# Gate and up projections: the low parts of two token operands of each run, made by GpSimd instead of VectorE

## The chip, the cores and the metric

The kernel runs on one core of a Trainium2 chip. The metric is the device time of one execution, in microseconds (us); less is better.

## The reference, cut to what matters

The reference is one layer of a hybrid decoder: a 2048-token prompt and eight single decode tokens go through a combined projection, three groups of heads, an output projection, and a SwiGLU feed-forward block. Everything is in float32. The change lies in the first half of the feed-forward block:

```python
def swiglu(h, w_gate, w_up, w_down):
    return (jax.nn.silu(h @ w_gate) * (h @ w_up)) @ w_down
```

Here `h` has 2056 rows (2048 prompt tokens and 8 decode tokens) of 1024, and `w_gate` and `w_up` are 1024 x 2816.

## The kernel before, in words

The kernel is a row of stages: `project_all`, `attend`, `combine`, `gate_up`, `down`. Each stage has one instruction stream for each engine, written out by hand, and semaphores between them; an engine works strictly in the order of its stream. A barrier stands between stages.

**Split products.** TensorE multiplies in a reduced float format (F32R). So each operand is split in a high part (a copy rounded by ScalarE) and a low part (the operand minus its high part, by VectorE or GpSimd), and each product is three matmuls: high times high, high times low, low times high.

**Seven products.** `gate_up` computes each 2 x 2 block product with seven smaller products of sums of blocks. They are called, in their order, b11, t2, t3, t1, b21, t4, b22 (m = 0 to 6). Each has a weight operand (a block of 512 x 128, or a combination of blocks) and a token operand. The seven token operands are A11, S2, S3, S1, A12, A22 and a second S2 (the variable `source_of`); S1 to S3 are sums, and the last one, made by the step called s4, overwrites S2. Each token operand is 4 x W columns on 128 partitions, with W = 344, 344 and 340.

**Runs.** The 2056 tokens are worked in three runs of those widths. A run has 22 steps g: gate and up for each of 11 pairs of column blocks. In every step TensorE does 7 products of 12 matmuls. A run's token operands are made once, at its beginning, and used by all its 22 steps. The first run's are made in the opening of the stage; those of the second and third run at a turn, in the last step of the run before (g = 21 and g = 43; `turn` in VectorE's stream).

**What each engine does in a step.** ScalarE makes the high parts of the next step's weights (`base_hi`, L2435 and L2436, and `combos_hi`, L2426) and copies the first product out (L2465). At a turn it also makes the seven high token parts (`tokens_hi`, L2451), the seventh after s4. VectorE makes low parts of weights (`combos_lo`, L2488, and `base_lo`, L2498), adds the products up (L2548, L2554, L2565, and L2510 in `quarter`), multiplies gate and up (L2514), and makes sums for the next stage (`act_sums`, L2523 to L2531); at a turn it makes the seven low token parts between these (`tokens_lo`, L2503). GpSimd makes the rest of the low weight parts (`base_lo`, L2403), the weight combinations of the step after next (`combos`, L2390, L2391, L2393, L2395), and at a turn then s4 (L2324). SyncE issues the loads and the stores.

TensorE waits, in the first step of a run (`i == 0`), for the low token part of each product. VectorE's order at a turn is: low part 0, quarter t1, low part 1, quarter b21 with its sums, low part 2, quarter t4 with its sums, low part 3, quarter b22 with its sums, low parts 4, 5 and 6. In the opening it is: low part 0, weights, low parts 1, 2, 3, then s4 (on VectorE this time), low parts 4, 5, 6; GpSimd does `combos(1)` meanwhile.

Of the kernel before, what the change touches and what calls it, by code (L numbers as in the profile page):

```python
# [14 lines left out]
F32 = mybir.dt.float32  # L15
# [3 lines left out]
ALU = mybir.AluOpType  # L19
# [980 lines left out]
def attend(nc, c, a, io, scratch, dec, key_of, cache, last_page, y_first, first_root):  # L1000
# [12 lines left out]
    units, items, phase_of, phase_start = [], {}, {}, []  # L1013
    slot = 0
    for own, work in attention_phases():
        span = len(own) or len(work) + 3
        phase_start.append((slot, len(units)))
        units_at = len(units)
        for after, item in work:
            items.setdefault(slot + after, []).append(item)  # L1020
            phase_of[item] = units_at
        if not own:
            first_unit = slot + span
        units += own
        slot += span
# [100 lines left out]
    with ExitStack() as ctx:  # L1126
# [4 lines left out]
        names = ("low_zeroed in_turned q_copied0 q_copied1 q_copied2 q_copied3 k_hi in_hi in_lo turned t_hi t_lo pv scored min made probs v_hi v_lo o_copied o_ready inverted o_out row_made row_out "  # L1131
                 "q0 q1 k0 k1 v0 v1 decay page0 page1 page2 weighed halved added st0 st1 st2 st3 row_st0 row_st1 "
                 "raised conv_w_in conv_in0 conv_in1 conv_step conved conv_out w_ahead gain_ahead fox_ahead mem_ahead first_squares first_var first_root first_normed")
        with stage(nc, names) as (block, s):
# [11 lines left out]
            for n in range(SLOTS_ALL):  # L1146
                m = unit_at(n)
# [6 lines left out]
                if u:  # L1154
                    k = chunk_index[u.head, u.ch]
# [459 lines left out]
def combine(nc, c, io, scratch, dec, first, y_first, first_root, stock):  # L1615

    N = NT + 1
    SAMP = NT  # L1620
# [531 lines left out]
WIDTHS = (344, 344, 340)  # L2152
# [84 lines left out]
def gate_up(nc, c, io, scratch, raw, stock):  # L2237
# [14 lines left out]


    SC, ITEMS, M = len(WIDTHS), 2 * PAIRS, len(ORDER)
    N = SC * ITEMS
    W = max(WIDTHS)
    H = DT // 2
    with ExitStack() as ctx:
        sb, psum = alloc(ctx, nc)
        h_hi, h_lo = sb("h_hi", [P, M, H, W], F32R), sb("h_lo", [P, M, H, W], F32R)  # L2260
# [5 lines left out]
        last_out = last_results(stock)  # L2266
        ps = psum("ps_gate_up", [P, 8, BLK])
        source_of = (A11, S2, S3, S1, A12, A22, S2)
        names = ("w_in0 w_in1 t_step t_made t_hi t_lo b_hi b_lo d_lo a11_in h_in s_step h_hi h_lo b_first done p1 u2 u3 u4 c22 c11 c21 c12 silu "
                 "quarter summed act stored sum_stored s_stored ahead")  # L2270
        with stage(nc, names) as (block, s):
            w_in = (s.w_in0, s.w_in1)
# [25 lines left out]
            def product(g, name):  # L2298
                return ps[:, (M * g + ORDER.index(name)) % 8, 0:width(g)]

            def shape(ap):
                return ap.rearrange("p m d n -> p (m d) n")

            def s_combo(eng, sc, name):

                n = WIDTHS[sc]
                x = [part[:, i, :, 0:n] for i in range(6)]
                step = 4 * sc - 3
                if name == "s1":
                    eng.wait_ge(s.h_in, 48 * sc)  # L2310
                    eng.wait_ge(s.a11_in, 16 * sc)
                    eng.tensor_tensor(x[S1], x[S3], x[A22], ALU.add).then_inc(s.s_step, 1)
                elif name == "s2":
                    eng.wait_ge(s.s_step, step + 1)
                    eng.tensor_tensor(x[S2], x[S1], x[A11], ALU.subtract).then_inc(s.s_step, 1)
                elif name == "s3":
                    eng.wait_ge(s.s_step, step + 2)
                    eng.tensor_tensor(x[S3], x[A11], x[S3], ALU.subtract).then_inc(s.s_step, 1)
                else:

                    if sc:
                        eng.wait_ge(s.s_step, step + 3)
                    eng.wait_ge(s.h_lo, M * sc + 2)
                    eng.tensor_tensor(x[S2], x[A12], x[S2], ALU.subtract).then_inc(s.s_step, 1)  # L2324

            @block.sync
            def _(sp):
                def weights(g):
                    if g >= N:
                        return  # L2330

                    if g >= 3:
                        sp.wait_ge(s.b_lo, g - 2)
                    sp.wait_ge(s.d_lo, g - 1)
                    sp.dma_start(raw[:, g % 2], gate_up_weights(io, g)).then_inc(w_in[g % 2], 16)

                def tokens(sc):

                    sp.wait_ge(s.h_lo, M * sc)
                    if sc == SC - 1:  # L2340
                        sp.wait_ge(c.last_h, LAST_STORES)
                    load_tokens(sp, scratch, stock, sc, s.a11_in, s.h_in)

                def down_ahead():

                    pile, acts, _ = down_buffers(stock)
                    sp.wait_ge(s.h_lo, M * SC)
                    for j in range(PILE):
                        sp.dma_start(pile[:, j, :], down_rows(io.w_down)[:, 0, j, 0:BLK]).then_inc(s.ahead, 16)
                    sp.dma_start(acts[0], scratch.act_c[KEPT.index(PASSES[0]), 0]).then_inc(s.ahead, 16)  # L2350

                for g in range(N):
                    if g == 0 or is_up(g):
                        weights(g + 2)
                    if is_up(g):
                        weights(g + 3)
                    if g % ITEMS == 2 and g // ITEMS + 1 < SC:
                        tokens(g // ITEMS + 1)
                    if g == 2 * ITEMS + 9:
                        sp.wait_ge(s.stored, stored_before(2 * PAIRS))  # L2360
                        sp.wait_ge(s.sum_stored, stored_before(2 * PAIRS))
                        down_ahead()
                    if is_up(g) and g < N - 1:
                        j = g % ITEMS // 2
                        sp.wait_ge(s.act, g // 2 + 1)
                        for p, at, t, n in run_pieces(g // ITEMS):
                            dst = scratch.act_c[0:3, p, :, j, at:at + n].rearrange("m p t -> p m t")
                            sp.dma_start(dst, sums_of(g)[:, :, t:t + n]).then_inc(s.sum_stored, 16)
                        for p, at, t, n in run_pieces(g // ITEMS):
                            dst = scratch.act_c[3:7, p, :, j, at:at + n].rearrange("m p t -> p m t")  # L2370
                            sp.dma_start(dst, out_of(g)[:, :, t:t + n]).then_inc(s.stored, 16)
                        if g // ITEMS == SC - 1:
                            sp.dma_start(scratch.act_s[:, j].rearrange("p s (a t) -> p (s a) t", a=2),
                                         act_out[:, :, all_but_sample(g):width(g)]).then_inc(s.s_stored, 16)
                sp.wait_ge(s.stored, stored_before(N // 2 - 1))
                sp.wait_ge(s.sum_stored, stored_before(N // 2 - 1))
                sp.wait_ge(s.s_stored, 16 * (PAIRS - 1))
                sp.wait_ge(s.ahead, 16 * (PILE + 1))

            @block.gpsimd  # L2380
            def _(pool):
# [15 lines left out]
                def base_lo(g):  # L2397
# [4 lines left out]
                    at = SLOT["b11"]  # L2402
                    pool.tensor_tensor(shape(lo[:, at:at + 2]), b[:, :, 0:P], shape(hi[:, at:at + 2]).bitcast(F32), ALU.subtract).then_inc(s.b_lo, 1)  # L2403

                combos(1)
                for g in range(N):
                    base_lo(g + 1)
                    combos(g + 2)
                    sc, i = g // ITEMS + 1, g % ITEMS
                    if sc < SC:  # L2410
                        if i in (8, 12, 16):
                            s_combo(pool, sc, ("s1", "s2", "s3")[(i - 8) // 4])
                        if i == ITEMS - 1:
                            s_combo(pool, sc, "s4")

            @block.scalar
            def _(act):
# [65 lines left out]
            def _(dve):  # L2483
# [14 lines left out]
                    dve.tensor_tensor(w_lo[:, g % 2, last], raw[:, g % 2, H:DT, P:2 * P], w_hi[:, g % 2, last].bitcast(F32), ALU.subtract).then_inc(s.d_lo, 1)  # L2498

                def tokens_lo(sc, m):  # L2500
                    n = WIDTHS[sc]
                    dve.wait_ge(s.h_hi, M * sc + m + 1)
                    dve.tensor_tensor(h_lo[:, m, :, 0:n], part[:, source_of[m], :, 0:n], h_hi[:, m, :, 0:n].bitcast(F32), ALU.subtract).then_inc(s.h_lo, 1)  # L2503

                def quarter(g, name, base, which, read):

# [28 lines left out]
                combos_lo(0)  # L2535
                dve.tensor_tensor(w_lo[:, 0, SLOT["b22"]], raw[:, 0, H:DT, P:2 * P], w_hi[:, 0, SLOT["b22"]].bitcast(F32), ALU.subtract).then_inc(s.d_lo, 1)
                tokens_lo(0, 1)
                tokens_lo(0, 2)
                tokens_lo(0, 3)
                s_combo(dve, 0, "s4")  # L2540
                for m in range(4, M):
                    tokens_lo(0, m)
                for g in range(N):
                    n, b, q = width(g), g % 2, g // 2
# [25 lines left out]
                    quarter(g, "b21", first[:, b, 0:n], 0, s.c11)  # L2570
                    if is_up(g):
                        act_sums(g, 0)
                    if turn:
                        tokens_lo(turn, 2)
                    quarter(g, "t4", u3[:, 0:n], 1, s.c21)
                    if is_up(g):
                        act_sums(g, 1)
                    if turn:
                        tokens_lo(turn, 3)
                    dve.wait_ge(s.u4, g + 1)  # L2580
                    quarter(g, "b22", u2[:, b, 0:n], 2, s.c12)
                    if is_up(g):
                        act_sums(g, 2)
                    if turn:
                        for m in range(4, M):
                            tokens_lo(turn, m)

            @block.tensor
            def _(pe):
                for g in range(N):  # L2590
# [7 lines left out]
                    for m, name in enumerate(ORDER):  # L2598
# [2 lines left out]
                        if g == 0 and name == "b22":  # L2601
                            pe.wait_ge(s.d_lo, 1)
                        if i == 0:
                            pe.wait_ge(s.h_lo, M * sc + m + 1)
                        if m == 0 and g >= 2:

                            pe.wait_ge(s.c12, g - 1)
# [525 lines left out]
```

## Time and profile before

| | |
|---|---|
| three timed runs | 2769.03, 2776.25 and 2781.96 us; median 2776.25 us |
| the profiled execution's own time | 2769.61 us |
| its span, first to last instruction | 2767.9 us |
| mean granted TensorE clock | 0.98 |
| the stage `gate_up` in the span | from about 1403 to about 2312 us |

The span lies within 1.7 us of the profiled execution's own time. Times in the rows below are in us from the start of the span, those marked ns apart. A busy engine is one with an instruction in flight, and an instruction's time holds what it waited for once it had begun.

### The profile page before, as it was taken

To read this page: it belongs to the slowest core of one execution; us is meant where nothing else is said; L and a number is where in the kernel's file an instruction comes from. 1 tells how busy PE (TensorE), PEld (TensorE's weight loads), DVE (VectorE), ACT (ScalarE), POOL (GpSimd) and SP (SyncE) were. 2 spreads that over 40 slices of the span, in tenths; PEclk is the share of its full clock that TensorE was granted. 3 is DMA by queue.
4 is the path that set the end of the run, shared out by engine and by line. 5 is a ranking of instruction groups with operands and counts; after the bars stand their busy time and mean duration, and the time that the engine had idled before them with its cause. 6 is when DMAs were issued, how large, how long until landed. Compare 5 with 4: busy or idle time off the path is not lost. (4 is left out here: it accounts for less than half of the span.)

```text
span 2767.9 us, 42326 instructions
## 1 busy us (share of the span) xinstructions
PE 2632.1 (95%) x14745; PEld 2377.2 (86%) x14745; DVE 1935.7 (70%) x2560; ACT 1169.0 (42%) x2012; POOL 1694.4 (61%) x963
## 2 busy tenths in 40 slices
PE   8999989889999998899979999999989999999998
PEld 7999889877777777677879999999989997887887
DVE  5366696478888887676577778878787875445664
ACT  4212321367777777633343333333433332223343
POOL 3486678488999998655556675666666660222232
PEclk9999999989999999999989999999999999999999
DMA  6588789566666677776635433543434546754564
GB/s 210 167 266 253 252 268 319 170 178 169 176 176 172 176 185 194 214 251 197 203 78 182 133 112 115 168 130 113 130 112 129 172 118 191 243 178 168 185 221 141
DMA packets 471365, 499.21 MB, mean 180 GB/s; under 512 B 172123, under 2 KB 359446, under 8 KB 470122
## 3 DMA queue, kind: packets, MB, share of 16 engines
q1 hardware_dynamic: 449730, 469.97, 56.3%
q10 hardware_dynamic: 21136, 25.50, 2.7%
q8 instruction: 118, 1.93, 0.3%
q0 software_dynamic: 288, 1.05, 0.1%
q14 instruction: 93, 0.76, 0.1%
HBM read 398.07 MB, written 94.16 MB: 178 GB/s over the span
## 5 line engine op out<-in xcount | busy, mean ns | idle before, releaser
L2613 PE MATMUL ps_gate_up<-h_hi,w_hi 128*128 128x344 f32 (+1 forms) x1848 | 593.7, 321 | 26.2 <-DVE h_lo L2503 14.2
L2615 PE MATMUL ps_gate_up<-h_hi,w_lo 128*128 128x344 f32 (+1 forms) x1848 | 594.0, 321 | 0.0
L2614 PE MATMUL ps_gate_up<-h_lo,w_hi 128*128 128x344 f32 (+1 forms) x1848 | 593.4, 321 | 0.0
L2613 PEld LDWEIGHTS ps_gate_up<-h_hi,w_hi 128*128 128x128 f32 x1848 | 349.9, 189 | 29.7 <-DVE h_lo L2503 16.4
L2614 PEld LDWEIGHTS ps_gate_up<-h_lo,w_hi 128*128 128x128 f32 x1848 | 350.2, 190 | 0.0
L2615 PEld LDWEIGHTS ps_gate_up<-h_hi,w_lo 128*128 128x128 f32 x1848 | 350.1, 189 | 0.0
L878 PE MATMUL ps_proj<-w_hi,h_hi 128*128 128x428 f32 (+1 forms) x800 | 289.3, 362 | 10.0 <-ACT proj_out L602 9.9
L879 PE MATMUL ps_proj<-w_lo,h_hi 128*128 128x428 f32 (+1 forms) x800 | 285.4, 357 | 0.0
L880 PE MATMUL ps_proj<-w_hi,h_lo 128*128 128x428 f32 (+1 forms) x800 | 284.9, 356 | 0.0
L1595 DVE TENSOR_TENSOR p_lo<-ps_turned,p_hi 128x512 fp32r<-128x512 f32 (+1 forms) x352 | 211.0, 614 | 81.5 <-ACT p_hi L1483 80.0
L2390 POOL TENSOR_TENSOR stock<-common 128x512 f32<-128x512 f32 x65 | 104.2, 1602 | 251.0 <-DVE w_lo L2488 235.9
L3009 PE MATMUL ps_down<-wd_hi,act_hi 128*128 128x512 f32 x616 | 241.6, 392 | 6.3 <-DVE wd_lo L2917 6.3
L2807 POOL TENSOR_TENSOR stock<-common 128x512 f32<-128x512 f32 x55 | 82.1, 1501 | 265.7 <-DMA common<-in_w_down 265.6
L3011 PE MATMUL ps_down<-wd_hi,act_lo 128*128 128x512 f32 x616 | 240.7, 391 | 0.0
L3010 PE MATMUL ps_down<-wd_lo,act_hi 128*128 128x512 f32 x616 | 240.7, 391 | 0.0
L1483 ACT ACTIVATE p_hi<-ps_turned 128x512 fp32r<-128x512 f32 (+1 forms) x352 | 185.8, 538 | 129.0 <-PE ps_turned L1420 91.7
L1420 PE MATMUL ps_turned<-ident,probs 128*128 128x128 f32 x1216 | 195.7, 278 | 25.0 <-DVE p_lo L1595 8.9
L2855 ACT ACTIVATE act_hi<-stock 128x768 fp32r<-128x768 f32 (+2 forms) x114 | 83.1, 774 | 302.5 <-PE ps_down L3011 288.7
L1420 PEld LDWEIGHTS ps_turned<-ident,probs 128*128 128x128 f32 x1216 | 145.8, 142 | 67.1 <-DVE p_lo L1595 16.4
L2403 POOL TENSOR_TENSOR w_lo<-common,w_hi 128x1024 fp32r<-128x1024 f32 x65 | 162.5, 2500 | 64.2 <-ACT w_hi L2436 64.2
L2933 DVE TENSOR_TENSOR acc<-acc,ps_down 128x512 f32<-128x512 f32 x96 | 62.4, 684 | 198.0 <-PE ps_down L3011 198.0
L2488 DVE TENSOR_TENSOR w_lo<-stock,w_hi 128x2048 fp32r<-128x2048 f32 x66 | 165.3, 2504 | 19.2 <-ACT w_hi L2426 19.0
(346 smaller groups left out, 6574.3 us busy)
## 6 DMA issues: line engine op xcount, KB each, us to landing
stock<-in_cache_k SPq DMA_DIRECT2D x192, 256.0 KB, 3.4
common<-in_cache_v SPq DMA_DIRECT2D x172, 256.0 KB, 3.1
stock<-act_combined SPq DMA_DIRECT2D x56, 704.0 KB, 4.2
common<-in_w_gate SPq DMA_DIRECT2D x33, 1024.0 KB, 5.3
common<-in_w_up SPq DMA_DIRECT2D x33, 1024.0 KB
common<-in_w_down SPq DMA_DIRECT2D x44, 512.0 KB, 5.8
page_v<-in_cache_v SPq DMA_DIRECT2D x84, 256.0 KB, 3.1
common<-in_w_in SPq DMA_DIRECT2D x44, 428.0 KB, 4.9
```

Of the source, the lines that this page charges most:

```text
L878: pe.matmul(ps[:, bank, 0:w], a_hi, w_hi[:, d, :], start=(j == 0 and d == 0), stop=False)
L879: pe.matmul(ps[:, bank, 0:w], a_hi, w_lo[:, d, :], start=False, stop=False)
L880: mm = pe.matmul(ps[:, bank, 0:w], a_lo, w_hi[:, d, :], start=False, stop=(j == 3 and d == 1))
L1420: turned = pe.transpose(out[:, r * P:(r + 1) * P], probs(u.head, QCH * u.ch + r, u.j * P, (u.j + 1) * P), c.ident[:])
L1483: act.activation(a.p_hi[:, m % PARTS, r0 * P:], ps_t[:, bank_of["unit", m], r0 * P:], ACT.Copy).then_inc(s.t_hi, 1)
L1595: dve.tensor_tensor(a.p_lo[:, m % PARTS, r0 * P:], ps_t[:, bank_of["unit", m], r0 * P:], a.p_hi[:, m % PARTS, r0 * P:].bitcast(F32), ALU.s ...
L2613: pe.matmul(acc, a_hi, h_hi[:, m, d, 0:n], start=d == 0, stop=False)
L2614: pe.matmul(acc, a_hi, h_lo[:, m, d, 0:n], start=False, stop=False)
L2615: mm = pe.matmul(acc, a_lo, h_hi[:, m, d, 0:n], start=False, stop=d == H - 1)
L3009: pe.matmul(out, a_hi[:, n % 2, j, :], w_hi[:, slot, :], start=first, stop=False)
L3010: pe.matmul(out, a_hi[:, n % 2, j, :], w_lo[:, slot, :], start=False, stop=False)
L3011: mm = pe.matmul(out, a_lo[:, n % 2, j, :], w_hi[:, slot, :], start=False, stop=end)
```

## The change

In each run, the low token parts of the third and fifth product (m = 2 and m = 4, operands S3 and A12) are made by GpSimd in place of VectorE. They get a semaphore of their own, `h_lo_pool`, and whoever waited for `h_lo` with a count now waits for the semaphore and the count that `low_made` gives. At a turn GpSimd does: `combos(g + 2)`, low part 2, s4, low part 4. In the opening it does low parts 2 and 4 ahead of `combos(1)`. VectorE does all its other work in the same order as before.

```diff
-        span = len(own) or len(work) + 3
+        span = len(own) or max(at for at, _ in work) + 4
...
+    POOL_PARTS = (2, 4)
+    DVE_LATE = [m for m in (4, 5, 6) if m not in POOL_PARTS]
...
+            def low_made(sc, m):
+
+                if m in POOL_PARTS:
+                    return s.h_lo_pool, len(POOL_PARTS) * sc + POOL_PARTS.index(m) + 1
+                own = [k for k in range(M) if k not in POOL_PARTS]
+                return s.h_lo, len(own) * sc + own.index(m) + 1
+
+            def low_of(eng, sc, m):
+
+                n = WIDTHS[sc]
+                eng.wait_ge(s.h_hi, M * sc + m + 1)
+                return eng.tensor_tensor(h_lo[:, m, :, 0:n], part[:, source_of[m], :, 0:n], h_hi[:, m, :, 0:n].bitcast(F32), ALU.subtract)
...
-                    eng.wait_ge(s.h_lo, M * sc + 2)
+                    eng.wait_ge(*low_made(sc, 1))
...
-                    sp.wait_ge(s.h_lo, M * sc)
+                    for m in (POOL_PARTS[-1], M - 1):
+                        sp.wait_ge(*low_made(sc - 1, m))
...
+                def tokens_lo(sc, m):
+
+                    low_of(pool, sc, m).then_inc(s.h_lo_pool, 1)
+
+                for m in POOL_PARTS:
+                    tokens_lo(0, m)
                 combos(1)
...
                         if i == ITEMS - 1:
+                            tokens_lo(sc, POOL_PARTS[0])
                             s_combo(pool, sc, "s4")
+                            tokens_lo(sc, POOL_PARTS[1])
...
-                tokens_lo(0, 2)
-                tokens_lo(0, 3)
+                for m in (2, 3):
+                    if m not in POOL_PARTS:
+                        tokens_lo(0, m)
                 s_combo(dve, 0, "s4")
-                for m in range(4, M):
+                for m in DVE_LATE:
                     tokens_lo(0, m)
...
-                    if turn:
+                    if turn and 2 not in POOL_PARTS:
                         tokens_lo(turn, 2)
...
-                        for m in range(4, M):
+                        for m in DVE_LATE:
                             tokens_lo(turn, m)
...
                         if i == 0:
-                            pe.wait_ge(s.h_lo, M * sc + m + 1)
+                            pe.wait_ge(*low_made(sc, m))
```

## Rows read from the trace of the kernel before

**Rows 1.** The page, part 1: busy us, share, instructions of each engine.

```profile
PE 2632.1 (95%) x14745; PEld 2377.2 (86%) x14745; DVE 1935.7 (70%) x2560; ACT 1169.0 (42%) x2012; POOL 1694.4 (61%) x963
```

**Rows 2.** Waits of TensorE, whole span: us in total, times, longest us.

```profile
PE ps_gate_up L2613 <- DVE h_lo L2503: 14.2, 6, 4.0
```

**Rows 3.** Timeline, TensorE, first turn: start, us, work, idle before and releaser.

```profile
1710.12 0.32 PE L2613 MATMUL ps_gate_up<-h_hi,w_hi 128*128 128x344 f32 x1
...
1712.80 0.32 PE L2615 MATMUL ps_gate_up<-h_hi,w_lo 128*128 128x344 f32 x1
1717.07 0.66 PE L2613 MATMUL ps_gate_up<-h_hi,w_hi 128*128 128x344 f32 x1 [3.95 <-DVE h_lo L2503]
1717.53 0.49 PE L2614 MATMUL ps_gate_up<-h_lo,w_hi 128*128 128x344 f32 x1
...
1720.39 0.49 PE L2615 MATMUL ps_gate_up<-h_hi,w_lo 128*128 128x344 f32 x1
1722.72 0.65 PE L2613 MATMUL ps_gate_up<-h_hi,w_hi 128*128 128x344 f32 x1 [1.83 <-DVE h_lo L2503]
...
1732.73 0.40 PE L2613 MATMUL ps_gate_up<-h_hi,w_hi 128*128 128x344 f32 x1 [0.47 <-DVE w_lo L2498]
```

**Rows 4.** Timeline, VectorE, first turn.

```profile
1710.58 0.50 DVE L2510 TENSOR_TENSOR act<-stock,ps_gate_up 128x344 f32<-128x344 f32 x1
...
1712.21 3.30 DVE L2523 TENSOR_TENSOR silu<-act 128x344 f32<-128x344 f32 x1
1715.44 1.58 DVE L2503 TENSOR_TENSOR h_lo<-stock,h_hi 128x1376 fp32r<-128x1376 f32 x1
...
1717.48 0.52 DVE L2514 TENSOR_TENSOR act<-act,silu 128x344 f32<-128x344 f32 x1
...
1718.58 2.58 DVE L2527 TENSOR_TENSOR act<-act 128x344 f32<-128x344 f32 x1
1721.08 1.58 DVE L2503 TENSOR_TENSOR h_lo<-stock,h_hi 128x1376 fp32r<-128x1376 f32 x1
...
1724.66 4.59 DVE L2503 TENSOR_TENSOR h_lo<-stock,h_hi 128x1376 fp32r<-128x1376 f32 x3
...
1731.79 0.68 DVE L2498 TENSOR_TENSOR w_lo<-common,w_hi 128x512 fp32r<-128x512 f32 x1
```

**Rows 5.** Timeline, GpSimd, first turn.

```profile
1709.29 2.52 POOL L2395 TENSOR_TENSOR stock<-common,stock 128x512 f32<-128x512 f32 x1
1711.76 3.38 POOL L2324 TENSOR_TENSOR stock<-stock 128x1376 f32<-128x1376 f32 x1
1718.07 2.71 POOL L2403 TENSOR_TENSOR w_lo<-common,w_hi 128x1024 fp32r<-128x1024 f32 x1 [2.93 <-ACT w_hi L2436]
```

**Rows 6.** Timelines of the opening: ScalarE, VectorE, GpSimd, TensorE.

```profile
1407.62 6.29 ACT L2451 ACTIVATE h_hi<-stock 128x1376 fp32r<-128x1376 f32 x5
...
1410.56 7.84 DVE L2503 TENSOR_TENSOR h_lo<-stock,h_hi 128x1376 fp32r<-128x1376 f32 x3
...
1410.12 1.66 POOL L2390 TENSOR_TENSOR stock<-common 128x512 f32<-128x512 f32 x1 [11.71 <-DVE w_lo L2488]
...
1430.65 0.39 PE L2613 MATMUL ps_gate_up<-h_hi,w_hi 128*128 128x344 f32 x1 [2.15 <-DVE w_lo L2498]
```

**Rows 7.** Timeline, ScalarE, first turn.

```profile
1700.73 6.31 ACT L2451 ACTIVATE h_hi<-stock 128x1376 fp32r<-128x1376 f32 x5
...
1715.18 1.35 ACT L2451 ACTIVATE h_hi<-stock 128x1376 fp32r<-128x1376 f32 x1 [6.29 <-POOL stock L2324]
```

**Rows 8.** Windows (busy us of each engine, then PEclk) and TensorE's first matmul in `down`.

```profile
2019.00:2020.00 1.00, 0.93 (x4) 0.93 (x5) 0.96 (x3) 1.00 (x3) 0.00 (x0) 0.76 0.00 0
2022.00:2023.00 1.00, 0.48 (x2) 0.04 (x1) 1.00 (x1) 0.13 (x1) 0.78 (x1) 0.53 0.00 0
...
2314.17 0.76 PE L3009 MATMUL ps_down<-wd_hi,act_hi 128*128 128x512 f32 x1 [5.00 <-DVE wd_lo L2917]
...
2318.00:2320.00 2.00, 2.00 (x6) 1.51 (x6) 2.00 (x4) 1.11 (x3) 0.00 (x0) 0.53 1.22 266
```

More of the change, by code:

```diff
@@ L2268, in gate_up @@
         source_of = (A11, S2, S3, S1, A12, A22, S2)
-        names = ("w_in0 w_in1 t_step t_made t_hi t_lo b_hi b_lo d_lo a11_in h_in s_step h_hi h_lo b_first done p1 u2 u3 u4 c22 c11 c21 c12 silu "
+        names = ("w_in0 w_in1 t_step t_made t_hi t_lo b_hi b_lo d_lo a11_in h_in s_step h_hi h_lo h_lo_pool b_first done p1 u2 u3 u4 c22 c11 c21 c12 silu "
                  "quarter summed act stored sum_stored s_stored ahead")
@@ L2346, in down_ahead @@
                     pile, acts, _ = down_buffers(stock)
-                    sp.wait_ge(s.h_lo, M * SC)
+                    for m in (POOL_PARTS[-1], M - 1):
+                        sp.wait_ge(*low_made(SC - 1, m))
                     for j in range(PILE):
@@ L2500, in tokens_lo @@
                 def tokens_lo(sc, m):
-                    n = WIDTHS[sc]
-                    dve.wait_ge(s.h_hi, M * sc + m + 1)
-                    dve.tensor_tensor(h_lo[:, m, :, 0:n], part[:, source_of[m], :, 0:n], h_hi[:, m, :, 0:n].bitcast(F32), ALU.subtract).then_inc(s.h_lo, 1)
+                    low_of(dve, sc, m).then_inc(s.h_lo, 1)
                 def quarter(g, name, base, which, read):
@@ L2577, in _ @@
                         act_sums(g, 1)
-                    if turn:
+                    if turn and 3 not in POOL_PARTS:
                         tokens_lo(turn, 3)
```

## The prediction

> **What bounds the kernel now.** I read the page first: TensorE is busy 95% of the span, VectorE 70%, GpSimd 61% [rows 1]. So the time can change only where TensorE waits, or where it runs at the lower clock. The view of TensorE's waits says where that touches the change: six waits for low token parts, 14.2 us together [rows 2], beside a few for low weight parts. The timeline puts them in three places: the opening of the stage (1407 to 1431), the first turn (1713 to 1733) and the second (302 us later, the same instructions with the same durations within 0.1 us). That sum is all that a better placing of this work could give back, with the slow clock that the pauses bring. Within 0.5% (13.9 us) this kernel's runs can't tell a change from none.
>
> At the first turn TensorE has done m = 1 by 1713.1 and starts m = 2 at 1717.07, as soon as VectorE has made its low part (1715.44 + 1.58). It starts m = 3 at 1722.72, after the next low part, and the next step at 1732.73, after VectorE's L2498 [rows 3, 4]. Its matmuls start every 0.158 us at full clock (17 steps from 1710.12 to 1712.80) and every 0.286 us at half clock (10 steps from 1717.53 to 1720.39) [rows 3].
>
> The rows to look at longest are VectorE's L2523 and L2527. Both are subtractions or sums on 344 columns, worth 0.52 us like L2514 [rows 4]. L2523 takes 3.30 us, from 1712.21 to 1715.51, and GpSimd's s4 ends at 1715.14; L2527 takes 2.58 us, to 1721.16, and GpSimd's L2403 ends at 1720.78 [rows 4, 5]. Each ends 0.37 us after the GpSimd instruction. VectorE's L2510, with one input in PSUM, takes 0.50 us in the midst of GpSimd's L2395 [rows 4, 5]. So a VectorE instruction with both inputs in SBUF and a GpSimd instruction exclude each other, for the whole length of the one that has begun, and instructions with a PSUM input go free. GpSimd pays as well: the three low parts of the opening take VectorE 7.84 us beside GpSimd's `combos(1)`, and 4.59 us alone at the turn [rows 4, 6].
>
> The Trainium skill has the same rule (SBUF — State Buffer, Who interferes with whom): a VectorE instruction with two SBUF inputs contends with a GpSimd instruction that reads SBUF, and the one that issues second waits for the other's end. The trace agrees: 3.30 us where 0.52 is the work. The rule speaks against this change, whose moved instruction reads SBUF twice; by it the sum is the one below, and without it the sum would be that of the second rival.
>
> **The moved work and its price.** A low token part is 1.53 us on VectorE (4.59 for three) [rows 4]. GpSimd's price isn't in the rows; the nearest is s4, of the same 128 x 1376 and two SBUF inputs, 3.38 us of which 0.37 was waiting behind L2514: 3.0 us [rows 5]. From L2403, 2.71 us for 1024 columns with a wait of about 0.48 (it began at 1718.07, and L2525 held VectorE until 1718.55), 2.23 us scale to 3.0 too. I take 3.0, with 2.9 and 3.4 as ends. So 3.1 us leave VectorE at each of the three places and 6.0 come to GpSimd, in time that the two share.
>
> **A turn, step by step.** Up to GpSimd's L2395 nothing changes. Then, in us after 1700:
> - GpSimd takes low part 2 where it took s4, its high part being there (ScalarE's five end at 7.0 [rows 7]): 11.8 to 15.1. TensorE starts m = 2 at 15.2 in place of 17.1, a gain of 1.9, and ends it at 17.1 to 18.3, as the clock falls or not.
> - VectorE's L2523 waits as before, to 15.5. GpSimd's s4 gets the port next: 15.5 to 18.5.
> - VectorE now goes on with L2510 (free, to 15.9) and L2514, which waits for s4: it runs 18.5 to 18.9. GpSimd's low part 4: 18.9 to 21.9.
> - VectorE's L2525 waits behind that: 21.9 to 22.2. GpSimd's L2403, whose ScalarE input follows s4's high part (18.5 + 1.35 + 1.0 + 0.5 = 21.4, by [rows 7] and the 2.9 us from L2451 to L2403 in [rows 5, 7]), comes next: 22.2 to 24.5.
> - VectorE's L2527 waits behind that: to 24.8. Low part 3: 24.8 to 26.3. It was there at 22.7 before [rows 4].
>
> TensorE is done with m = 2 by 18.3 and has nothing until 26.4: low part 4 was ready at 21.9, but it belongs to a later product. From 26.4 four products are left, 48 matmuls, 7.6 us at full clock, to 34.0. VectorE meanwhile needs 2.0 us to the next low part, as before (22.66 to 24.66), then two of them where it had three (3.1 in place of 4.6), and ends L2498 at 34.6 where it was 32.5: 2.1 us later [rows 4]. The clock decides which of the two comes last. After a pause of 4.0 us it fell in both turns, and at the beginning of `down`, after 5.0 us, it stayed at half from 2314.2 to about 2319.9 (the window from 2318 has 0.53) [rows 3, 8]. In the second turn it was at half for only about 3.4 us, from 2019.5 to 2022.9 (the mean of 2019 to 2020 is 0.76, that of 2022 to 2023 0.53) [rows 8]. After a pause of 8 us it will be at half: 3.4 us of it cost 3.4 x (1 - 0.158 / 0.286) = 1.5 us, 5.7 us cost 2.55. So TensorE ends the step between 35.5 and 36.5, and the next begins then in place of 32.7: 2.8 to 3.8 us lost. The second turn loses the same. Both together: 5.6 to 7.6.
>
> **The opening.** GpSimd sat idle until 1410.12 [rows 6], so its two low parts look free; they are not. In us after 1400: high part 2 is there at 10.1 (the second of five from 7.6 [rows 6]), and VectorE has a 0.7 us subtraction until 10.6. Then they alternate: GpSimd low part 2, 10.6 to 13.6; VectorE low part 1, to 15.1 (13.3 before, behind L2390, which ended at 11.8); GpSimd low part 4, to 18.1; VectorE low part 3, to 19.6; L2390, to 20.9; VectorE s4, to 22.4; L2391, to 23.6; VectorE low part 5, to 25.1; L2393, to 26.4; VectorE low part 6, to 27.9; L2395, to 29.1. ScalarE's L2426 (1.9 us) needs that last combination: 31.1. Before, `combos(1)` began at 1410.1 and, at some 2.5 us for each of four, was done by 1420, so this was hidden. GpSimd's L2403 holds the port to 31.4, VectorE's L2488 runs to 33.6 and L2498 to 34.2; TensorE starts step 1 at 34.4 in place of 30.65 [rows 6], 3.7 us later, after a pause of over 4 us, with 1.5 to 2.55 of slow clock: 5.2 to 6.3 us lost.
>
> **What costs nothing.** The edit in `attend` changes nothing: the only phase without units has 12 items in slots 0 to 11, so 12 + 3 and 11 + 4 are both 15. SyncE waits twice where it waited once, but for parts long made (the loads of the next run's tokens come two steps into a run). The stores of the turn's results come 3.7 us later; VectorE waits for the first of them before its L2510 of b21 in step 22, some 7 us after L2531. What they need to land no row here shows; if they were late, VectorE's chain has 0.9 to 1.9 us in hand behind TensorE's (34.6 against 35.5 to 36.5). VectorE is busy for 70% of the span [rows 1], so what it is late it catches up in the next steps, but TensorE's loss stays.
>
> **The sum.** 5.2 to 6.3 and 5.6 to 7.6 make 10.8 to 13.9 us; I take 12. Against the profiled execution that is 2769.6 + 12 = 2781.6; against the median of the runs, which lies 6.6 us above it, 2788.
>
> **The rivals.**
> - As summed, with 9 to 16 us: chance 0.60.
> - The clock stays at half through all 48 matmuls of a turn (13.7 us in place of 7.6), or a store or the weight chain adds a wait: 6.1 per turn in place of 1.5 to 2.55, so 18 to 23 us, 2794 to 2799. For it: in the first turn the clock was low from about 1715.7 to 1725.8, through two pauses [rows 3]. Against: it came back in 5.7 us of `down`. Chance 0.17.
> - The other side: GpSimd's new instruction doesn't hold VectorE up. Then at a turn low part 3 is ready before TensorE has done m = 2, s4 ends at 18.2 with its high part at 19.5, L2498 ends by 24.5, and TensorE, going through from 15.2 with five products (9.5 us), starts the next step at 24.7: 8 us gained per turn, up to 3 in the opening, 2757 to 2760. It decides if L2514 and L2525 of the turn take 0.5 us with GpSimd running. [rows 4, 5] are against it. Chance 0.04.
> - The port goes over in another order (VectorE gets two instructions for one of GpSimd's). If L2525 goes straight behind L2514, one wait of 2.2 us goes per turn, low part 3 is there at 24.1, and a turn costs 0.5 to 1.5 us; with less in the opening too, the whole is 2 to 9 us, 2778 to 2785. Against it: where both waited, L2395, L2514, s4, L2523 took turns one by one [rows 4, 5]. Chance 0.15.
> - It makes no difference, as the pause is only split otherwise (within 2 us): 0.04.
>
> **The numbers.** The likeliest case gives 2788. Slower by over 0.5% is above 2790: the second case whole (0.17) and some four tenths of the first (0.25), 0.42 together; faster by over 0.5% is 0.04; the rest, 0.54, is within. For eight in ten, the range goes from the lower edge of the case of the other port order, less 3 for the spread of the medians, 2775, to 2799, the upper edge of the slow-clock case.
>
> **What the profile would show.** TensorE's wait for m = 2 ends near 1715.2 with GpSimd as releaser, and a new wait for VectorE's h_lo of 7 to 9 us begins before m = 3, in both turns. VectorE's L2514, L2525 and L2527 in each turn take 2 to 3.5 us each. GpSimd's low parts take 3.0 to 3.5 us. In the opening `combos(1)` ends near 1429 and the wait for L2498 is 4 us or more. I am wrong if L2525 takes 0.5 us beside GpSimd, or if low part 3 is there before 1724.

## The result and the profile after

Over 20 runs of each kernel the median went from 2769.68 us to 2781.51 us. The ratio is 1.0037, with a 95% interval of 1.0026 to 1.0049: on 2769.7 us that is 10.2 us slower, between 7.2 and 13.6; the two medians lie 11.8 us apart, inside the same interval. The forecast was 12 us slower. Its 2788 was built on a median of three runs, 2776.25; twenty runs put that 6.6 us lower, beside the profiled execution.

The profiled execution of the changed kernel has a span of 2774.1 us, 6.2 us more than before. That isn't the size of the effect either. The view of one line's instructions gives where the stage begins and ends: the first matmul in `gate_up` and the first in `down`. In the kernel before:

```profile
L2613 PE MATMUL ps_gate_up<-h_hi,w_hi x1848: 313/319/656, 1407.3 to 2308.5; 128*128 128x344 f32 x124, 128*128 128x340 f32 x61
L3009 PE MATMUL ps_down<-wd_hi,act_hi x616: 389/389/764, 2314.2 to 2760.0; 128*128 128x512 f32 x154
```

In the changed kernel (24 lines further down):

```profile
L2637 PE MATMUL ps_gate_up<-h_hi,w_hi x1848: 313/319/656, 1402.2 to 2314.9; 128*128 128x344 f32 x124, 128*128 128x340 f32 x61
L3033 PE MATMUL ps_down<-wd_hi,act_hi x616: 389/389/763, 2320.5 to 2766.2; 128*128 128x512 f32 x154
```

The stage was 2314.2 - 1407.3 = 906.9 us long and is 2320.5 - 1402.2 = 918.3 us: 11.4 us more. `down` is as it was (453.7 and 453.6 us to the end of the span), and the stage happened to begin 5.1 us earlier, through stages that the change doesn't touch. Further down, a second profile of each kernel tells how well the stage's length repeats.

TensorE's waits in the stage, changed kernel (us in total, times, longest), beside [rows 2]:

```profile
PE ps_gate_up L2637 <- DVE h_lo L2314: 16.7, 2, 9.0
...
PE ps_gate_up L2637 <- DVE w_lo L2523: 4.2, 1, 4.2
PE ps_gate_up L2637 <- POOL h_lo L2314: 4.1, 2, 2.1
```

Six short waits for low token parts, 14.2 us, have become two long ones, 16.7 us, and two for GpSimd, 4.1 us. The timeline of the first turn, TensorE, VectorE and GpSimd, is what [rows 3 to 5] were before. Everything here is 0.61 us later in the span (1700.58 against 1699.97 for the first sum of step 21). L2314 is the low token part, on either engine; L2537 is the former L2514, L2546 to L2550 the former L2523 to L2527, L2339 is s4, L2420 the former L2403, L2523 the former L2498.

```profile
1715.81 0.42 PE L2637 MATMUL ps_gate_up<-h_hi,w_hi 128*128 128x344 f32 x1 [2.07 <-POOL h_lo L2314]
...
1726.96 0.66 PE L2637 MATMUL ps_gate_up<-h_hi,w_hi 128*128 128x344 f32 x1 [8.98 <-DVE h_lo L2314]
```

```profile
1712.83 3.30 DVE L2546 TENSOR_TENSOR silu<-act 128x344 f32<-128x344 f32 x1
1716.05 0.50 DVE L2533 TENSOR_TENSOR act<-u,ps_gate_up 128x344 f32<-128x344 f32 x1
1716.58 2.90 DVE L2537 TENSOR_TENSOR act<-act,silu 128x344 f32<-128x344 f32 x1
1719.52 3.30 DVE L2548 TENSOR_TENSOR silu<-act 128x344 f32<-128x344 f32 x1
1722.85 2.55 DVE L2550 TENSOR_TENSOR act<-act 128x344 f32<-128x344 f32 x1
1725.32 1.58 DVE L2314 TENSOR_TENSOR h_lo<-stock,h_hi 128x1376 fp32r<-128x1376 f32 x1
...
1734.52 0.69 DVE L2523 TENSOR_TENSOR w_lo<-common,w_hi 128x512 fp32r<-128x512 f32 x1
```

```profile
1712.38 3.37 POOL L2314 TENSOR_TENSOR h_lo<-stock,h_hi 128x1376 fp32r<-128x1376 f32 x1
1715.72 3.39 POOL L2339 TENSOR_TENSOR stock<-stock 128x1376 f32<-128x1376 f32 x1
1719.08 3.37 POOL L2314 TENSOR_TENSOR h_lo<-stock,h_hi 128x1376 fp32r<-128x1376 f32 x1
1722.40 2.63 POOL L2420 TENSOR_TENSOR w_lo<-common,w_hi 128x1024 fp32r<-128x1024 f32 x1
```

Read the last two side by side. GpSimd runs four instructions without a pause. VectorE has four small instructions on 344 columns in the same time, each 0.52 us of work. L2546, L2537, L2548 and L2550 each end 0.37 or 0.38 us after the end of one of GpSimd's: 1716.13 after 1715.75, 1719.48 after 1719.11, 1722.82 after 1722.45, 1725.40 after 1725.03. Only L2533, which reads PSUM, takes its own 0.50 us. Low part 3 is thus ready at 1726.90. TensorE started m = 2 early, finished it, and stood for 8.98 us.

### The profile page after: what moved, and what is told of

Same layout as the page of the kernel before. It is cut to its first block and busy times, and to the rows that moved or that the text cites. A ratio compares the mean times of both kernels' runs of the same rounds, so it can differ in the third digit from the quotient of the medians.

```text
span 2774.1 us, 42328 instructions
## 1 busy us (share of the span) xinstructions
PE 2628.2 (95%) x14745; PEld 2374.9 (86%) x14745; DVE 1943.1 (70%) x2554; ACT 1169.8 (42%) x2012; POOL 1717.0 (62%) x969
## 5 line engine op out<-in xcount | busy, mean ns | idle before, releaser
L2637 PE MATMUL ps_gate_up<-h_hi,w_hi 128*128 128x344 f32 (+1 forms) x1848 | 594.6, 322 | 36.2 <-DVE h_lo L2314 16.7
L2420 POOL TENSOR_TENSOR w_lo<-common,w_hi 128x1024 fp32r<-128x1024 f32 x65 | 160.7, 2472 | 61.4 <-ACT w_hi L2461 61.4
L2460 ACT ACTIVATE w_hi<-common 128x1024 fp32r<-128x1024 f32 x66 | 69.4, 1052 | 254.8 <-PE ps_gate_up L2639 254.8
```

The lines of the kernel that those rows point to most:

```text
L2637: pe.matmul(acc, a_hi, h_hi[:, m, d, 0:n], start=d == 0, stop=False)
```

## The experiments

Each kernel's stage length, from the first matmul of `gate_up` to the first of `down`, is taken from its one profile. It is split at the first sum of step 21 and of step 43 (the line L2548 of before), which lie just ahead of the two turns: 292.7 us, 302.1 us and 312.1 us before. The columns give what each part is longer or shorter than that, from rounded times, so within 0.1 us; the last column is the timed ratio to the kernel before with its 95% interval (twenty runs of the changed kernel, six of the one with the sums late and s4 on VectorE, 10 to 12 of the others).

| kernel | stage, us | opening | first turn | second turn | ratio |
|---|---|---|---|---|---|
| before | 906.9 | | | | |
| before, again | 906.9 | 0.0 | 0.0 | 0.0 | one run |
| changed | 918.3 | +5.7 | +3.2 | +2.5 | 1.0037 (1.0026 to 1.0049) |
| changed, again | 918.1 | +5.6 | +3.2 | +2.4 | one run |
| turns only | 914.0 | +1.6 | +3.2 | +2.4 | 1.0012 (0.9997 to 1.0027) |
| opening only | 913.7 | +5.6 | +1.2 | 0.0 | 1.0010 (0.9994 to 1.0026) |
| part 2 only | 911.9 | +1.8 | +1.6 | +1.6 | 1.0016 (1.0002 to 1.0030) |
| part 4 only | 914.0 | +3.2 | +2.0 | +1.9 | 1.0022 (1.0009 to 1.0034) |
| written only | 901.1 | -0.6 | -3.7 | -1.5 | 0.9965 (0.9951 to 0.9979) |
| s4 on VectorE | 905.0 | +0.1 | -0.9 | -1.1 | 0.9983 (0.9973 to 0.9993) |
| and L2403's work | 902.9 | -0.6 | -1.6 | -1.8 | 0.9983 (0.9969 to 0.9998) |
| sums late | 920.1 | +1.6 | +5.5 | +6.2 | 1.0031 (1.0016 to 1.0047) |
| sums late, s4 on VectorE | 916.8 | 0.0 | +4.3 | +5.5 | 1.0055 (1.0038 to 1.0072) |
| sums at the end, s4 on VectorE | 908.0 | +1.6 | -1.0 | +0.5 | 0.9994 (0.9978 to 1.0011) |

**Both kernels again.** No edit.

> The kernel before unaltered, a second profile: the stage 906.9 us again within 1 us (with the clock's falls placed otherwise, within 2 us), while its beginning (1407 us in the first profile) may move by several us.

> The changed kernel unaltered, a second profile. If the stage's length is a property of the kernel, it is 918.3 us again within 1 us, wherever the stage begins in the span (1402 us in the first profile).

The lengths came back within 0.2 us, 906.9 and 918.1, though the second profile of the changed kernel begins the stage at 1405.2 and not at 1402.2. The stage's beginning lay anywhere between 1400.9 and 1415.3 us over all the profiles of this study, in kernels that are alike up to there. Between the two profiles of the changed kernel the span grew by 4.5 us: 3.0 us of it lie ahead of the stage and 1.7 us in `down`. The stage's length is the sharper measure, but it is one execution of each kernel, and the next experiment shows what the clock can add to it.

**Turns only, opening only.** The set of moved parts is made to depend on the run: none in the first (turns only, shown here), or in the first alone (opening only, `((2, 4), (), ())`).

```diff
-    POOL_PARTS = (2, 4)
+    PARTS = ((), (2, 4), (2, 4))
...
```

The lines left out make the counts and the conditions follow this set.

> GpSimd makes low parts 2 and 4 at the two turns only; the opening is as before. In the profile the gate_up stage (TensorE's first matmul in it to its first in down) was 906.9 us before and 918.3 us with the change. If the three places add up independently, the opening's 5.7 us come back: 912 to 913 us, 5 to 7 us above before in the timed runs, and each turn again has TensorE waiting some 9 and 8 us for low part 3. If instead the loss were one of the whole program (where the code lies, clock, other stages), the stage would stay near 918.

> Low parts 2 and 4 on GpSimd in the opening only; the turns are as before. If the port that VectorE and GpSimd take turns on is the cause, step 1 starts 3 us later than before and then runs at half clock for some us: the stage is 912 to 913 us (906.9 + 5.7). If a GpSimd that was idle costs nothing, as the opening's idle 11.7 us suggest, the stage is 907 us.

Both stages are a little longer than expected, 914.0 and 913.7, and 7.1 + 6.8 is 13.9 and not 11.4. The columns tell why. The turns-only kernel loses 3.2 and 2.4 us at its turns, as the changed kernel does, and the opening-only kernel loses 5.6 us in its opening, as the changed kernel does; these make 11.2 us. What is too much lies where the kernels are unaltered: 1.6 us in the opening of the one, 1.2 us in the first turn of the other. Windows of the turns-only kernel's opening, with PEclk the third number from the end:

```profile
1437.30:1439.30 2.00, 0.64 (x4) 0.67 (x5) 1.97 (x4) 0.00 (x0) 1.24 (x1) 1.00 0.00 0
1439.30:1441.30 2.00, 2.00 (x11) 2.00 (x10) 1.87 (x5) 1.43 (x4) 2.00 (x3) 0.64 0.64 175
1441.30:1443.30 2.00, 2.00 (x9) 2.00 (x9) 0.00 (x0) 2.00 (x4) 1.92 (x2) 0.51 1.00 347
1443.30:1445.30 2.00, 2.00 (x14) 2.00 (x14) 0.52 (x1) 1.96 (x2) 2.00 (x2) 1.00 0.01 2
```

After the pause before step 1 the clock fell to half for about 3.4 us (the means 0.64 and 0.51 of two windows), and the same instructions with the same pause, 2.15 us, kept the full clock in the kernel before. A fall that comes or doesn't is worth about 1.5 us here. The two differ earlier too. This is TensorE's first matmul of m = 1, about 6.1 us into the stage, in the kernel before and in the turns-only kernel:

```profile
1413.33 0.62 PE L2613 MATMUL ps_gate_up<-h_hi,w_hi 128*128 128x344 f32 x1 [2.26 <-issue]
```

```profile
1421.32 0.40 PE L2638 MATMUL ps_gate_up<-h_hi,w_hi 128*128 128x344 f32 x1 [2.26 <-issue]
```

At 0.62 us the clock was still at half there, at 0.40 us it was back at full. Seven profiles have this opening unaltered: the four with 0.62 or 0.63 us kept the stage's opening within 0.1 us of before, the three with 0.40 us (turns only, sums late, sums at the end) lost 1.6 us. What decides when the clock comes back there isn't shown. The timed ratios, 3.3 and 2.8 us with intervals of some 4 us to each side, don't contradict 5.6 and 5.6, but can't confirm them.

**Part 2 only, part 4 only.** The same edit with `((2,), (2,), (2,))` and `((4,), (4,), (4,))`.

> Only low part 2 on GpSimd, everywhere; part 4 stays on VectorE. Taking turns on the port, by durations of the trace: at a turn m = 2 starts 1.9 us earlier, low part 3 is there at about 21.5 (22.7 before), and the next step starts 0 to 1 us later than before; in the opening step 1 starts 2 to 3 us later, with no fall of the clock. Stage 909.5 to 911.5 us, 3 to 4 us above before. If what counts were only how much work GpSimd is given (half of it), it would be half of the change's 11.4 us in the stage: 912.6.

> Only low part 4 on GpSimd, everywhere. By the port theory it is the dearer half although TensorE needs part 4 later: at a turn it comes straight behind s4 and holds up VectorE's low part 2, so m = 2 starts near 20.1 (17.1 before) and low part 3 is there near 25.3 (22.7 before): 1.7 us per turn and up to 1.5 more where the clock stays low; in the opening step 1 starts 2 to 3 us later. Stage 913 to 916 us. By the amount of moved work alone it would be 912.6, as with part 2.

Part 4 alone gave 914.0, inside what was expected; part 2 alone gave 911.9, 0.4 above its upper end. The amount moved is the same, and the losses are 5.0 and 7.1 us. Part 2 missed at the turns: TensorE started m = 3 1.2 us earlier, as expected, but the clock fell in the pause of 4.2 us before it, and the next step began 1.6 us later at the first turn where 0 to 1 was expected, 1.3 us after the low weight parts it needs were ready. Part 4 shows its mechanism in VectorE's timeline of the first turn (L2311 is the low token part there):

```profile
1712.64 3.31 DVE L2545 TENSOR_TENSOR silu<-act 128x344 f32<-128x344 f32 x1
1715.88 4.48 DVE L2311 TENSOR_TENSOR h_lo<-stock,h_hi 128x1376 fp32r<-128x1376 f32 x1
```

GpSimd goes from s4 straight to low part 4, which TensorE needs two products later; VectorE's low part 2, which TensorE is waiting for, takes 4.48 us for 1.5 us of work. TensorE's pause before m = 2 is 6.9 us in place of 3.95, and m = 2 and m = 3 start within 0.2 us of where they were expected.

**Written only.** GpSimd stays as busy, but reads nothing for these parts.

```diff
-                    low_of(pool, sc, m).then_inc(s.h_lo_pool, 1)
+                    pool.wait_ge(s.h_hi, M * sc + m + 1)
+                    for k in range(3):
+                        if k:
+                            pool.wait_ge(s.zeroed, 2 * (2 * sc + (m == 4)) + k)
+                        pool.memset(h_lo[:, m, :, 0:WIDTHS[sc]].bitcast(F32), 0.0).then_inc(s.zeroed if k < 2 else s.h_lo_pool, 1)
```

> In place of low parts 2 and 4 GpSimd writes zeros to them, three times over, so that it is busy for a similar time but reads nothing from SBUF; left out are these two low parts of the token operands. If a GpSimd instruction holds VectorE up only because both read through one port, VectorE's multiplication and sums (0.52 us of work) take 0.5 us beside the writes where they took 2.9 and 3.3, low part 3 at a turn is there 4 us or more earlier than with the change, and the stage is 904 us or less. If any GpSimd instruction holds VectorE up, or the loss comes from GpSimd being slow or in the wrong order, they take as long as the writes do and the stage stays within 2 us of 918.

901.1 us, and a ratio of 0.9965: 17.2 us less than the changed kernel in the stage. TensorE starts m = 3 of the first turn 7.5 us earlier than with the change (4 or more were expected). GpSimd and VectorE in the first turn (L2428 the three writes, L2339 s4; L2541 to L2554 the small instructions):

```profile
1708.65 3.85 POOL L2428 MEMSET h_lo<- 128x1376 f32 x3
1712.46 3.72 POOL L2339 TENSOR_TENSOR stock<-stock 128x1376 f32<-128x1376 f32 x1
```

```profile
1709.11 0.52 DVE L2550 TENSOR_TENSOR silu<-act 128x344 f32<-128x344 f32 x1
1709.54 0.51 DVE L2537 TENSOR_TENSOR act<-u,ps_gate_up 128x344 f32<-128x344 f32 x1
1710.08 0.52 DVE L2541 TENSOR_TENSOR act<-act,silu 128x344 f32<-128x344 f32 x1
1710.64 0.52 DVE L2552 TENSOR_TENSOR silu<-act 128x344 f32<-128x344 f32 x1
1711.19 0.52 DVE L2554 TENSOR_TENSOR act<-act 128x344 f32<-128x344 f32 x1
1711.62 1.58 DVE L2314 TENSOR_TENSOR h_lo<-stock,h_hi 128x1376 fp32r<-128x1376 f32 x1
...
1713.66 2.89 DVE L2541 TENSOR_TENSOR act<-act,silu 128x344 f32<-128x344 f32 x1
```

Beside 3.85 us of writes, four small instructions of VectorE with two SBUF inputs take their bare 0.52 us, and so does low part 3 (1.58 us), which begins beside the writes. Beside s4, which reads, the same L2541 takes 2.89 us. GpSimd's time for the part is longer than in the changed kernel (3.85 against 3.37 us), so its slowness isn't the cause. What costs is that it reads SBUF. This is also how the Trainium skill puts it (SBUF — State Buffer, Who interferes with whom): a VectorE instruction with two SBUF inputs contends with a GpSimd instruction that reads SBUF, not with one that only writes it; this run agrees, 0.52 us against 2.89 us.

**s4 on VectorE.** The kernel before, with work moved the opposite way.

```diff
-                        if i == ITEMS - 1:
-                            s_combo(pool, sc, "s4")
...
                     if turn:
                         tokens_lo(turn, 1)
+                        s_combo(dve, turn, "s4")
```

> The kernel before, with one SBUF-to-SBUF sum moved the other way: s4 is made by VectorE at the turns, behind low part 1, in place of GpSimd. By the port theory the two-input work is 1.5 us in place of 3.0 in the shared time, VectorE's L2523 no longer waits, and low parts 2 and 3 are there 0.5 to 1 us earlier: 1 us less per turn, stage 904 to 906 us. If VectorE's own load were what bounds a turn, 1.5 us more for it would make each turn 1.5 us longer: 910 us.

905.0 us, 0.9 and 1.1 us less at the turns, as expected, and the first kernel that leaves nothing out and is faster than the kernel before beyond its interval (0.9973 to 0.9993). The engine that had the most to do in this stretch was given more, and was done sooner.

**And L2403's work.** On top of it, VectorE makes the low parts of 1024 weight columns for the second step of each run, ahead of L2488.

> The kernel with s4 on VectorE, and one more two-input subtraction moved from GpSimd to VectorE: the low parts of 1024 weight columns for the second step of each run (L2403 of that step), made just ahead of L2488. On GpSimd it holds VectorE up by 2.1 us at each turn and 1.7 us in the opening; on VectorE it is 1.2 us of work. The port theory: 0.9 us less at each turn and 0.5 us less in the opening, stage 902 to 904 us (905.0 with s4 alone). If VectorE's load were the bound and not the port, 1.2 us more at each of three places: 908 to 909 us.

902.9 us, 0.6 us less in the opening and 0.7 us less at each turn than with s4 alone, where 0.5 and 0.9 were expected. This is VectorE's multiplication behind low part 2 in the first turn, with s4 alone on VectorE and with L2403's work there too:

```profile
1717.53 2.20 DVE L2512 TENSOR_TENSOR act<-act,silu 128x344 f32<-128x344 f32 x1
```

```profile
1718.75 0.52 DVE L2512 TENSOR_TENSOR act<-act,silu 128x344 f32<-128x344 f32 x1
```

In the first of the two GpSimd's L2403 runs beside it, in the second it doesn't. The timed ratio is 0.9983 again, with 0.9969 to 0.9998: faster than the kernel before, but the 2 us between these two kernels can't be told apart in whole runs.

**Sums late, with and without s4.** VectorE's order at a turn: low parts 1, 2, 3 together, parts 4, 5, 6 behind one quarter each, and the five sums for `down` (`act_sums`) after the next step's low weight parts.

```diff
                         base_lo(g + 1)
+                    if g and g % ITEMS == 0:
+                        for which in range(3):
+                            act_sums(g - 1, which)
...
                     if turn:
-                        tokens_lo(turn, 1)
+                        for m in (1, 2, 3):
+                            tokens_lo(turn, m)
...
```

> The kernel before, with VectorE's order at a turn changed: low parts 2 and 3 straight behind low part 1, low parts 4, 5, 6 behind one quarter each, and the five sums for the next stage after the next step's low weight parts. s4 stays on GpSimd. TensorE's waits for low parts 2 and 3 should fall from 3.9 and 1.8 us to under 3 together, and the next step should start 2 to 3 us earlier: stage 900 to 903 us. If the port is so full that order doesn't matter, it stays within 1 us of 906.9.

> As the run with the sums late, and s4 on VectorE behind low part 3. The port theory expects the least total time on the port: low parts 2 and 3 there before TensorE needs them, no fall of the clock at the turns, the next step starting at about 29.6 in place of 32.7: stage 898 to 901 us, 6 to 9 us below before. If only the order matters and not who makes s4, it equals the run with the sums late.

Both missed, by 17 and 16 us over the upper ends: 920.1 and 916.8. The theory had the turn right and stopped looking too early. Which of the two is the slower isn't settled: in the stage it is the one with s4 on GpSimd, in timed runs the other (1.0031 against 1.0055, and the intervals overlap). TensorE, first turn, in the kernel that has s4 on VectorE too:

```profile
1708.86 0.43 PE L2615 MATMUL ps_gate_up<-h_hi,w_hi 128*128 128x344 f32 x1 [0.19 <-DVE h_lo L2501]
...
1724.90 0.40 PE L2615 MATMUL ps_gate_up<-h_hi,w_hi 128*128 128x344 f32 x1 [1.28 <-DVE w_lo L2496]
...
1743.49 0.63 PE L2615 MATMUL ps_gate_up<-h_hi,w_hi 128*128 128x344 f32 x1 [3.89 <-DVE w_lo L2496]
```

SyncE's stores and loads, ScalarE and VectorE of the same stretch:

```profile
1731.30 1.47 SPq L2368 DMA_DIRECT2D act_combined<-silu  x3
1732.81 1.72 SPq L2371 DMA_DIRECT2D act_combined<-act  x3
1734.62 0.73 SPq L2335 DMA_DIRECT2D common<-in_w_up  x1
```

```profile
1734.66 0.51 DVE L2508 TENSOR_TENSOR silu<-stock,ps_gate_up 128x344 f32<-128x344 f32 x1 [2.00 <-DMA act_combined<-silu]
```

```profile
1736.45 1.04 ACT L2433 ACTIVATE w_hi<-common 128x1024 fp32r<-128x1024 f32 x1
```

The step after the turn does start 3.4 us earlier (1724.90 is 29.4 us after the first sum of step 21; 1732.73 was 32.8 [rows 3]), and 2.5 us earlier with s4 on GpSimd. But the sums now run beside GpSimd's `combos`, 6.7 us for 2.6 of work, the stores wait for them, VectorE waits 2.00 us for the stores, ScalarE's silu and then its high weight parts (1736.45) come behind VectorE, and TensorE waits 3.89 us one step later, with the clock at half behind it. What each link of this chain costs wasn't measured apart.

**Sums at the end.** One thing put otherwise: the five sums behind low part 6, in the turn's own step.

> The kernel with the sums late and s4 on VectorE, with one thing put otherwise: the five sums are made at the end of the turn's own step, behind low part 6, and not behind the next step's low weight parts. The runs with the sums late started the next step 3.4 us earlier and then waited 3.9 us one step later. If the late sums did that (the stores, the load queued behind them on SyncE, and ScalarE's work all come after them), the wait is gone here, the step after the turn starts 0 to 1 us earlier than before, and with a fall of the clock in the pause the stage is 905 to 910 us. If making the low parts early does the harm, the stage stays at 915 to 918 us.

908.0 us, as expected; the wait one step later is gone, so it was the late sums and what is queued behind them. The turns themselves are no better than with s4 alone (-1.0 and +0.5 us against -0.9 and -1.1), since the pause only lies elsewhere: low parts 2 and 3 come early, and TensorE waits 2.7 and 3.0 us at the end of the step for the weights. So an earlier place for the low parts gave nothing on top of s4, and a later place for the sums cost some 10 us at the two turns (+4.3 and +5.5 us against -1.0 and +0.5); what made a turn shorter was less time in which GpSimd and VectorE exclude each other.

## Why the prediction was right

**What bounds a turn: right.** Every step of the first turn came at the forecast time. In us after 1700, less the 0.61 us that this profile is later: m = 2 started at 15.20 (forecast 15.2), low part 3 was ready at 26.29 (26.3), m = 3 started at 26.35 (26.4), L2498's successor ended at 34.60 (34.6). GpSimd's price for a low part, taken from s4 less a wait at 3.0 us, shows as 3.37 with 0.4 us of waiting in it. Its remark that GpSimd pays as well rested on times of VectorE (7.84 and 4.59 us); it shows here, in that waiting.

**The clock: right at the first turn, a little low at the second.** It was at half when TensorE resumed at 1726.96 and came back at about 1731.4 (windows of the changed kernel):

```profile
1728.00:1730.00 2.00, 2.00 (x9) 2.00 (x9) 1.97 (x3) 0.00 (x0) 0.00 (x0) 0.50 0.03 10
1730.00:1732.00 2.00, 2.00 (x10) 2.00 (x10) 2.00 (x3) 0.00 (x0) 0.00 (x0) 0.64 1.02 278
```

That is 4.5 us at half, 2.0 us lost, between the forecast's 1.5 and 2.55. The turns cost 3.2 and 2.5 us, 5.7 together, where 5.6 to 7.6 was forecast. For each turn the forecast had 2.8 to 3.8 us, so the second lies below its range: TensorE's pause before m = 3 was 7.71 us there and not 8.98, and behind it the clock stayed at half for 3.1 us only. The pauses alone don't give these costs. TensorE's pauses in the first turn grew from 6.25 us [rows 3] to 11.05, by 4.8 us, and the next step began 3.3 us later: before, some 7 us of the turn's matmuls ran at half clock, and here 4.5. In the second turn the pauses grew by 1.7 us, from 8.1 to 9.8, and the next step began 2.6 us later.

**The opening: right in sum, with two small errors against each other.** TensorE in the opening:

```profile
1410.08 0.63 PE L2637 MATMUL ps_gate_up<-h_hi,w_hi 128*128 128x344 f32 x1 [4.09 <-issue]
...
1428.62 0.63 PE L2637 MATMUL ps_gate_up<-h_hi,w_hi 128*128 128x344 f32 x1 [4.17 <-DVE w_lo L2523]
```

The stage begins 5.1 us earlier here, so step 1 starts at 1433.7 on the scale of before, 3.05 us later than [rows 6] have it and not 3.7. The alternation was right one by one; GpSimd's four combinations ended 0.65 us sooner than summed, 28.45 in place of 29.1. The clock then stayed at half for 5.9 us, where 3.4 to 5.7 was forecast. 5.7 us lost; 5.2 to 6.3 was forecast. That the two errors nearly cancel is luck. An idle GpSimd was no cover: its idle time [rows 6] was not idle time of the port.

**What should cost nothing did.** `down` has its length, and VectorE's waits for stores didn't grow in the changed kernel. The remark that VectorE catches up in the next steps held there, but the kernels with the sums late show how little it takes to break it.

**The rivals.** That GpSimd's instruction doesn't hold VectorE up is refuted by the changed kernel. The run with writes comes nearest to what it would have been, with these parts left out: 901.1 us for the stage, a gain of 5.8 us where this rival had 16 to 19. There s4 and L2403's work, which read, still hold VectorE up. Another order of handing the port over is refuted by the four ends in the timeline above. The clock at half through all 48 matmuls didn't occur at either turn in the two profiles of the changed kernel.

**The whole.** 11.4 us in the stage, 10.2 (7.2 to 13.6) in timed runs, 12 forecast. The difference of 1.2 us between the two lies within the interval and isn't explained further.

## What to carry to other kernels

Before work is moved from VectorE to GpSimd because GpSimd is idle, look whether VectorE's neighbours in time have two SBUF inputs. If an instruction of VectorE ends some 0.4 us after one of GpSimd's, again and again, the two exclude each other; there the moved work costs its GpSimd duration to both (here 3.0 us where VectorE takes 1.53), and it can pay to move work the other way. And the length of TensorE's pauses isn't their cost: the clock at half behind them belongs to it, and it can add to the growth of the pauses (2.6 us for 1.7 at the second turn) or take from it (3.3 us for 4.8 at the first).

## What the hardware showed that was not expected

The same instructions with the same pause before step 1 kept TensorE's full clock in one profile and lost it for some 3 us in another, 1.6 us of time, with no difference in the instructions up to there; three of the kernels above have it in an unaltered opening (turns only, sums late, and sums at the end). In these three the clock had come back to full earlier in the stage, before m = 1, and the later fall followed; in the other four it came back at the end of m = 1 or in m = 2, and there was no fall behind step 1. And three writes of 128 x 1376 by GpSimd, 1.3 us each, cost VectorE's two-input instructions nothing at all, 0.52 us each beside them.
